# The lower parts of the weight chunks on GpSimd instead of VectorE, in the group loop of a hybrid encoder layer

## The reference

```
h   = RMSNorm(x) * (1 + scale1) + shift1
P   = h @ w_in  -> [z | xBC | dt | q | k | v | branch gates]
A   = Mamba-2 SSD branch (grouped heads, causal depthwise conv on x/B/C, chunked scan, SiLU gate, grouped RMSNorm)
B   = sliding-window attention branch (learned sinks, partial rotary)
m   = sigmoid(g_A) * (A @ w_ssm_out) + sigmoid(g_B) * (B @ w_att_out);   o = m @ w_out
x   = x + gate1 * RMSNorm(o)
h   = RMSNorm(x) * (1 + scale2) + shift2
[g | u] = h @ w_ffn_in;  g = causal depthwise conv (width 3) over positions
x   = x + gate2 * RMSNorm((silu(g) * u) @ w_ffn_out)
```

## Time and profile before

| | |
|---|---|
| median of 3 runs | 1462.64 us (1460.32 to 1465.84) |
| profiled execution | 1468.68 us, span 1466.9 us |
| TensorE busy, span share | 1365.2 us, 93% |
| VectorE busy | 772.5 us, 53% |
| ScalarE busy | 502.6 us, 34% |
| GpSimd busy | 405.6 us, 28% |
| mean granted clock of TensorE | 0.946 |

### The profile page before, as it was taken

The page is one execution under the profiler, slowest core; times in us unless marked ns, Lnnn a source line. Parts: engine busy times, 40 slices in busy tenths (PEclk is TensorE's granted clock), DMA queues, the critical chain, the costliest instruction groups (busy, mean ns, idle before and its releaser), DMA issues. The chain is left out here.

```text
span 1466.9 us, 24764 instructions
## 1 busy us (share of the span) xinstructions
PE 1365.2 (93%) x10355; PEld 1269.8 (87%) x10355; DVE 772.5 (53%) x1288; ACT 502.6 (34%) x888; POOL 405.6 (28%) x263
## 2 busy tenths in 40 slices
PE   4699998999999999999899999994899999999994
PEld 1488987898898998988889999993899999999993
DVE  1644414877887888778353000328566666650114
ACT  2212424363553553634323222333333333322221
POOL 0532310101101011011123444331444444443332
PEclk7599987999999999999999999996799999999997
DMA  9276624344245343341333222221222222222221
GB/s 373 101 259 223 198 77 120 104 127 141 70 136 147 89 123 116 118 131 45 113 119 132 87 87 87 101 82 38 74 87 87 87 87 87 87 74 91 88 68 62
DMA packets 68351, 165.83 MB, mean 113 GB/s; under 512 B 21160, under 2 KB 34376, under 8 KB 64768
## 3 DMA queue, kind: packets, MB, share of 16 engines
q1 hardware_dynamic: 68240, 164.25, 34.7%
HBM read 150.85 MB, written 13.83 MB: 112 GB/s over the span
## 5 line engine op out<-in xcount | busy, mean ns | idle before, releaser
L181 PE MATMUL psum<-hp_hi,w_hi 128*128 128x274 f32 x1488 | 458.7, 308 | 15.9 <-POOL hp_lo L298 11.7
L159 POOL TENSOR_TENSOR w_lo<-raw_w,w_hi 128x1024 fp32r<-128x1024 f32 x127 | 307.0, 2418 | 569.8 <-ACT w_hi L153 569.8
L181 PE MATMUL psum<-hp_lo,w_hi 128*128 128x274 f32 x1488 | 438.6, 295 | 0.0
L181 PE MATMUL psum<-hp_hi,w_lo 128*128 128x274 f32 x1488 | 438.1, 294 | 0.0
L153 ACT ACTIVATE w_hi<-raw_w 128x1024 fp32r<-128x1024 f32 x175 | 185.1, 1058 | 629.4 <-PE psum L181 576.5
L181 PEld LDWEIGHTS psum<-hp_hi,w_hi 128*128 128x128 f32 x1488 | 287.8, 193 | 35.7 <-issue 16.4
L181 PEld LDWEIGHTS psum<-hp_lo,w_hi 128*128 128x128 f32 x1488 | 290.7, 195 | 0.8
L181 PEld LDWEIGHTS psum<-hp_hi,w_lo 128*128 128x128 f32 x1488 | 288.9, 194 | 0.0
L181 PE MATMUL psum<-hq_hi,w_hi 128*128 128x274 f32 x832 | 248.1, 298 | 15.4 <-POOL hq_lo L1568 13.3
L181 PE MATMUL psum<-hq_hi,w_lo 128*128 128x274 f32 x832 | 244.9, 294 | 0.0
L181 PE MATMUL psum<-hq_lo,w_hi 128*128 128x274 f32 x832 | 244.6, 294 | 0.0
(11 more groups left out here) (235 smaller groups left out, 2018.9 us busy)
## 6 DMA issues: line engine op xcount, KB each, us to landing
raw_w<-in_w_grp SPq DMA_DIRECT2D x57, 512.0 KB, 3.8
raw_w<-in_w_ffn_in SPq DMA_DIRECT2D x44, 512.0 KB, 3.6
ada<-in_w_ada SPq DMA_DIRECT2D x12, 1024.0 KB, 20.3
ada_g<-in_w_ada SPq DMA_DIRECT2D x6, 2048.0 KB, 8.6
raw_w<-in_w_ffn_out SPq DMA_DIRECT2D x22, 512.0 KB, 3.5
acs_b<-mem_acs SPq DMA_DIRECT2D x8, 1096.0 KB, 7.1
raw_w<-in_w_ssm SPq DMA_DIRECT2D x16, 512.0 KB, 3.5
raw_w<-in_w_qkv SPq DMA_DIRECT2D x13, 512.0 KB, 6.7
```

What stands on the lines that cost most here:

```text
L159: eng.tensor_tensor(flat(w_lo[self.hl_slot(n)]), raw_w[self.raw_slot(n)][:], flat(w_hi[self.hl_slot(n)]).bitcast(F32), ALU.subtract).then_ ...
L181: mm = pe.matmul(out[:, h, :], w, x[:, cols], start=first and j == 0, stop=last and j == 2)
```

## The change

In the group loop GpSimd calls `split_lo` in VectorE's place. The three parts 1, 2 and 3 of a group stand right behind the copies of the tails, ahead of the first `xt`; part 4 stands ahead of the second `xt`, part 5 ahead of the fifth, part 6 behind it. Nothing else is moved: ScalarE's upper parts, SP's loads and TensorE's order are the same.

```diff
                             pool.tensor_copy(tails[:, 1], raw_last(TW)).then_inc(tail_s, 1)
+                            w.split_lo(pool, GT * g + 1)
+                            w.split_lo(pool, GT * g + 2)
+                            w.split_lo(pool, GT * g + 3)
                             for c in range(NC5 * g, NC5 * g + NC5):
                                 L, b = piece(c)[1], c % 2
+                                if c % NC5 == 1:
+                                    w.split_lo(pool, GT * g + 4)
+                                if c % NC5 == 4:
+                                    w.split_lo(pool, GT * g + 5)
                                 pool.wait_ge(xd_s, c + 1)
...
+                            w.split_lo(pool, GT * g + GT)
+                        w.all_split(pool)
...
                             at.evac_scores(dve, g, 1)
-                            w.split_lo(dve, GT * g + 1)
                             conv(g, 0)
...
                             at.normalise(dve, 0)
-                            w.split_lo(dve, GT * g + 2)
                             at.normalise(dve, 1)
...
                             silu(g, 1)
-                            w.split_lo(dve, GT * g + 3)
                             silu(g, 2)
...
                             weigh(c + 1)
-                            w.split_lo(dve, GT * g + 4)
                             out_y(c)
...
                             weigh(c + 4)
-                            w.split_lo(dve, GT * g + 5)
                             out_y(c + 3)
...
                             state(c + 4)
-                            w.split_lo(dve, GT * g + GT)
-                        w.all_split(dve)
```

## The result

| | before | changed |
|---|---|---|
| median of 4 runs | 1463.39 us (1460.32 to 1465.84) | 1495.89 us (1491.22 to 1500.57) |
| ratio, 95% interval | | 1.0216 (1.0187 to 1.0246) |
| profiled execution, span | 1466.9 us | 1496.9 us |
| VectorE / GpSimd busy | 772.5 / 405.6 us | 794.6 / 516.8 us |

A forecast was written before the change was run, and what follows sets the result against it. TensorE's own instructions were taken to bound the loop. Holds of 1.15 + 0.93 + 1.08 = 3.16 us a group, 25.3 us over eight, added to the runs' median of 1462.64 us, gave 1488 us, range 1470 to 1502.

The forecast's parts named there:

- The bound: Group loop: TensorE's own instructions bound it; shortening VectorE's way to the last scan product could win 5.7 us at most.
- First part: First lower part: GpSimd holds VectorE's convolution, so score evacuations and TensorE's token sums come 1.15 us late per group.
- Second part: Second lower part: GpSimd holds VectorE's scaling of the first scores, so TensorE's first turn comes 0.93 us late per group.
- Third, fourth and sixth part: These three lower parts: each hold is covered by slack or VectorE's idle time, so they cost nothing.
- Fifth part: Fifth lower part, between chunk products: VectorE's decays are held, making TensorE's last scan product 1.08 us later per group.
- Rival (a): Fifth part: GpSimd gets in only after all four decays; scan product about 0.35 us late, 1482 us; chance 0.17.
- When the held one goes on: At each hold: the trace shows the blocked instruction released 0.14 us before the holder's end, the page about 115 ns after.
- the prediction's 6 us more by the page: Release by the page's figure: each stall 0.25 us longer, 3 x 8 x 0.25 = 6 us more, time about 1494.
- The sum: All holds together: 1.15 + 0.93 + 1.08 = 3.16 us a group, 25.3 us over eight groups.
- The other side: Wherever both ask, VectorE goes ahead and GpSimd waits; the last scan product gains 5.7 us, 1457 us; chance 0.06.

The follow-up runs named there:

- e1: The changed kernel with the first lower part of each group back on VectorE, the other five on GpSimd: 1487.3 us.
- e6: The kernel before with only the third, fourth and sixth lower parts of each group moved to GpSimd: 1467.0 us, ratio 0.9996 to before.
- e4: The changed kernel with the fifth lower part of each group back on VectorE: 1484.1 us.
- e2: The kernel before with the first lower part of each group made twice on VectorE, nothing on GpSimd: 1483.5 us.
- e5: The kernel before with the fifth lower part, still on VectorE, moved behind the state update of the fourth piece: 1465.7 us, ratio 0.9999 to before.
- e7: The kernel before with parts 3, 4 and 6 on GpSimd and the fifth on VectorE behind the state update: 1466.0 us, ratio 0.9999.
- e10: The kernel before with each group's token sums in three parts, wide products between, and ScalarE's copy of their result behind the exponentials: 1464.8 us.
- e12: The kernel before with 4 of the 24 one-column products of each group's token sums: 1455.8 us, ratio 0.9927 to before.
- e8: The kernel before with an unused GpSimd difference of two SBUF operands added behind each group's first upper part: 1495.3 us.
- e9: The kernel before with an unused GpSimd fill with zeros of a 128x1024 tile added behind each group's first upper part: 1465.4 us.

## Why the prediction was right, point by point

- **The bound, and what the change could win.** Right: TensorE bound the loop, no wait for a lower part appeared, and VectorE's shorter queue won nothing.
- **First part, 1.15 us in each of 8 groups.** The token sums come 7.47 us after the group's second scores, 6.38 before: 1.09 us, in 7 groups. In the first group there was no such wait.
- **Second part, 0.93 us.** As a hold right (0.82 us by e1), as a term wrong: it was paid once, 0.7 us. In its place stands the term that the sum lacked, TensorE at half speed for a stretch: from the sums to the first turn 10.42 us in place of 8.91, 1.51 more, in a group that has one. This is the step that was off: I counted TensorE's waits and took its clock as given, though a stretch at half speed stood in two groups of the kernel before (from 309 and from 599 us).
- **Third, fourth and sixth part, nothing.** From the first to the third turn 6.54 us in both, from there to the first scan product 9.04 in both, from the last scan product to the next group's second scores 9.2 in both; and e6.
- **Fifth part, 1.08 us.** 17.86 us from first to last scan product became 18.89: 1.03. Rival (a), GpSimd passed over here, fell: the decays from 469.33 took 3.03 us with GpSimd from 469.51, so it got in after the first of them. e4 shows the price by taking it away (13.8 us of waits back to 5.7).
- **When the held one goes on.** The convolution's first instruction ended at 428.56, so its 0.79 us ran from 427.77, 0.21 us before GpSimd's end at 427.98. The Trainium skill ("SBUF — State Buffer", the section on a bandwidth-pool intuition that's wrong) puts it 115 ns behind the end, a figure that it measured on a DMA whose descriptors GpSimd writes, held by a VectorE copy. For the pair of this kernel the measurement decides, and the prediction's 6 us more by the page would have come nearer to the result for the wrong reason.
- **The sum.** 25.3 us were forecast, 16.2 came as waits and the rest by the clock. The forecast loop was right to a microsecond (25.9 by the two traces) by luck, through errors that cancel: 2 us too many at the first part (9.2 forecast, 7.4 paid, as the first group had no such wait), 7 at the second, half a microsecond at the fifth, against the 8 to 10 us lost at half speed that the sum did not have. The holds and two of the three places were foreseen, the clock was not. The whole kernel is 30 to 32 us slower; the 5.5 us behind the loop were not foreseen, and lie within the scatter of those stages.
- **The other side** (e), VectorE first wherever both ask, fell at the first place, for the reason given.

## What to carry to other kernels

An elementwise instruction moved from VectorE to GpSimd does not run beside all of VectorE's work: a VectorE instruction with two SBUF operands, or a tensor_scalar as here, stands still for the rest of GpSimd's twice as long instruction (or GpSimd's for VectorE's, where that came first), so ask at each place what is queued on VectorE in those microseconds and who waits for it. Three of the six places had room and cost nothing, three had none. And a wait on a TensorE that is otherwise busy can come with time at the lower clock that costs more than half as much again (e2: 8.6 us of waits, a loop 13.5 us longer), as a wait taken away can bring nothing.

## What the runs showed that I had not expected

- A wait of 1.2 us on TensorE before the token sums, made by VectorE alone, came with a kernel 18 us slower, 13.5 of them in the profiled loop, where the waits themselves are 8.6 (e2). Mean granted clock 0.948, was 0.954.
- Taking away eight waits of 0.71 us lowered the mean granted clock from 0.954 to 0.949 and 0.948 and left the time as it was (e5, e7: 12 runs each). What the clock goes by here stays open: the three profiles without a stretch in the groups (e10 to e12) point to the one-column products, and the times of e10 and e12 neither bear that out nor refute it.
- A GpSimd instruction that nobody waits for cost 30 us (e8), a fill of the same tile nothing (e9).
